# Stage seams of a hybrid decoder layer: order of the first tiles, who splits FFN2's first weights, and waits by chunk in the last down product

## What is computed

```
x = x + 0.5 * SwiGLU_1(rmsnorm(x))            # w_gate, w_up (1024 x 2816), w_down (2816 x 1024)
h = rmsnorm(x); p = h @ w_in                  # 72 column tiles of 128
A = sparse attention with an indexer's top-k; S = Mamba-2 SSD with gated RMSNorm
x = x + (sigmoid(ga) * (A @ w_attn_out) + sigmoid(gs) * (S @ w_ssd_out)) @ w_o
x = x + 0.5 * SwiGLU_2(rmsnorm(x))
```

## Time and profile before

| | |
|---|---|
| median of 3 runs | 3669.22 us (3666.39 to 3670.09) |
| the profiled execution | 3663.91 us |
| its span | 3661.7 us |
| PE busy | 3489.8 us, 95% |
| DVE busy | 2014.9 us, 55% |
| POOL busy | 1576.9 us, 43% |
| ACT busy | 764.0 us, 21% |
| mean granted clock of PE | 0.966 of 2.4 GHz |
| HBM | 74 GB/s over the span |

### The profile page before, as it was taken

How to read it: one execution, slowest core, us unless ns; L and a number is a source line. 1 busy time by engine, 2 the same in 40 slices (tenths; PEclk the granted TensorE clock), 3 DMA queues, 4 the chain that set the end, 5 groups by cost and what they waited for, 6 DMA issues and landing times.

```text
span 3661.7 us, 56375 instructions
## 1 busy us (share of the span) xinstructions
PE 3489.8 (95%) x22350; PEld 3271.4 (89%) x22350; DVE 2014.9 (55%) x2954; ACT 764.0 (21%) x1537; POOL 1576.9 (43%) x679
## 2 busy tenths in 40 slices
PE   7999999998999999999788889999999899999998
PEld 6999999988977999999667657779999899999998
DVE  5333333346666999987756636866273534334334
ACT  2000000012232111233665425651100200000000
POOL 3533433432322444444357417984443253353351
PEclk9999999999998999999799977999999999999999
DMA  2111111112211222232253326844151111111111
GB/s 85 56 46 34 53 50 34 52 40 76 56 29 58 92 91 91 79 98 92 67 53 105 106 67 176 233 119 150 49 172 50 29 58 40 40 57 40 40 57 52
DMA packets 399841, 272.29 MB, mean 74 GB/s; under 512 B 61843, under 2 KB 375523, under 8 KB 399721
## 3 DMA queue, kind: packets, MB, share of 16 engines
q1 hardware_dynamic: 379896, 225.75, 22.9%
q10 hardware_dynamic: 19824, 44.95, 3.3%
HBM read 211.05 MB, written 59.81 MB: 74 GB/s over the span
## 4 chain that ended last, share of the span: by engine, by line
PE 76%; DVE 15%; issue 3%; POOL 2%; ACT 1%; DMA 1%; another core or an unknown queue 0%; ACTq 0%; SPq 0%; DVEq 0%; POOLq 0%
PE setA L353 8%; PE setA L354 8%; PE setA L355 8%; PE setB L353 8%; PE setB L354 8%; PE setB L355 8%; DVE sc L1095 5%; DVE top L1093 5%; PE bankC L353 2%; PE bankC L355 2%; PE bankC L354 2%; PE bankD L355 2%; PE bankD L353 2%; PE bankD L354 2%; PE bankD L2054 1%
## 5 line engine op out<-in xcount | busy, mean ns | idle before, releaser
L345 POOL TENSOR_TENSOR whi<-wraw,ones 128x1024 fp32r<-128x1024 f32 x192 | 479.0, 2495 | 1669.6 <-PE setA L355 1095.3
L353 PE MATMUL setA<-hhi,whi 128*128 128x352 f32 (+1 forms) x2304 | 755.7, 328 | 40.0 <-POOL wlo L348 12.5
L353 PE MATMUL setB<-hhi,whi 128*128 128x352 f32 (+1 forms) x2304 | 750.0, 326 | 13.6 <-POOL wlo L348 13.6
L354 PE MATMUL setA<-hlo,whi 128*128 128x352 f32 (+1 forms) x2304 | 748.3, 325 | 0.0
L355 PE MATMUL setA<-hhi,wlo 128*128 128x352 f32 (+1 forms) x2304 | 747.1, 324 | 0.0
L354 PE MATMUL setB<-hlo,whi 128*128 128x352 f32 (+1 forms) x2304 | 745.3, 324 | 0.0
L355 PE MATMUL setB<-hhi,wlo 128*128 128x352 f32 (+1 forms) x2304 | 744.2, 323 | 0.0
L348 POOL TENSOR_TENSOR wlo<-wraw,whi 128x1024 fp32r<-128x1024 f32 x192 | 481.7, 2509 | 15.0
L353 PEld LDWEIGHTS setA<-hhi,whi 128*128 128x128 f32 x2304 | 438.6, 190 | 48.8 <-issue 30.6
L353 PEld LDWEIGHTS setB<-hhi,whi 128*128 128x128 f32 x2304 | 436.1, 189 | 18.2 <-POOL wlo L348 14.7
L354 PEld LDWEIGHTS setA<-hlo,whi 128*128 128x128 f32 x2304 | 438.5, 190 | 2.0
(11 more groups left out here) (413 smaller groups left out, 5503.8 us busy)
## 6 DMA issues: line engine op xcount, KB each, us to landing
wraw<-in_w_in SPq DMA_DIRECT2D x64, 512.0 KB, 3.7
wraw<-in_w_ffn_gate SPq DMA_DIRECT2D x44, 512.0 KB, 3.8
wraw<-in_w_ffn_up SPq DMA_DIRECT2D x44, 512.0 KB, 3.8
wraw<-in_w_ffn_down SPq DMA_DIRECT2D x44, 512.0 KB, 3.5
abc<-acsD SPq DMA_DIRECT2D x8, 2048.0 KB, 9.7
xcD<-cv ACTq DMA_DIRECT2D x24, 520.0 KB, 2.7
xc<-xcD SPq DMA_DIRECT2D x8, 1536.0 KB, 14.4
zD<-spill ACTq DMA_DIRECT2D x16, 524.0 KB, 2.7
```

The lines of the kernel that those rows point to most:

```text
L345: pool.tensor_tensor(dst_cols(slot, hi), dst_cols(slot), ones[:, :].unsqueeze(1).to_broadcast([P, KD, P]), ALU.mult).then_inc(w_hi, 1)
L353: pe.matmul(out, w1, r1, start=start, stop=False)
L354: pe.matmul(out, w1, r2, start=False, stop=False)
```

## The change

Four edits:

1. `gemm_pair` takes an order and the tile after which `between` is called. `after=0` in FFN1, FFN2 and w_in puts the sum of squares of chunk 2 between A0 and B0 instead of after B0.
2. In `pe_tail`, the first two tiles of both halves of w_ssd_out (s = 1, 2) run one after the other (A0 A1 A2 B0 B1 B2) by `gemm_tile`; those of w_o (s = 3) in the order A0 B0 A1 A2 B1 B2 (`FIRST_AHEAD`).
3. FFN2's first two weight tiles are split by ACT (`high_tile`, the rounded part) and DVE (`low_tile`, the rest) instead of POOL. ACT's two stand before and after the rounding of chunk 0, DVE's before and after its `hlo`. POOL waits until both are split and goes on with the third.
4. `pe_down_last` waits for the hidden tile chunk by chunk instead of for all of it.

```diff
--- before.py
+++ after.py
@@ -348,6 +348,18 @@
             pool.tensor_tensor(lo[:, slot, :], wraw[:, slot, :], hi[:, slot, :].bitcast(F32),
                                ALU.subtract).then_inc(w_split, 1)
 
+        def high_tile(act, n, half, slot, used):
+
+            act.wait_ge(raw_loaded[slot], half * 16 + 16)
+            act.wait_ge(*used)
+            act.activation(whi[:, slot, :], wraw[:, slot, :], ACT.Identity).then_inc(w_hi, 1)
+
+        def low_tile(v, n, slot):
+
+            v.wait_ge(w_hi, n + 1)
+            v.tensor_tensor(wlo[:, slot, :], wraw[:, slot, :], whi[:, slot, :].bitcast(F32),
+                            ALU.subtract).then_inc(w_split, 1)
+
         def products(pe, out, w1, w2, r1, r2, start, stop):
 
             pe.matmul(out, w1, r1, start=start, stop=False)
@@ -371,22 +383,24 @@
                     between(c)
 
 
-        def gemm_pair(pe, n, q, ready, between=None):
-
-            pe.wait_ge(w_split, n + 1)
-            for c, (o, w) in enumerate(CH):
-                if ready is not None:
+        ROUND = ((0, 0), (1, 0), (0, 1), (1, 1), (0, 2), (1, 2))
+        FIRST_AHEAD = ((0, 0), (1, 0), (0, 1), (0, 2), (1, 1), (1, 2))
+
+        def gemm_pair(pe, n, q, ready, between=None, order=ROUND, after=1):
+
+            for j, c in order:
+                o, w = CH[c]
+                if c == 0:
+                    pe.wait_ge(w_split, n + 1 + j)
+                if ready is not None and (j == 0 or order is not ROUND):
                     pe.wait_ge(ready[0], ready[1] + c + 1)
-                for j in range(2):
-                    if j and c == 0:
-                        pe.wait_ge(w_split, n + 2)
-                    if q:
-                        pe.wait_ge(gemm_evac[j], 3 * (q - 1) + c + 1)
-                    for k in range(KD):
-                        mm = products(pe, SETS[j][:, c, 0:w], whi[:, j, bass.ts(k, P)], wlo[:, j, bass.ts(k, P)],
-                                      hhi[:, k, o:o + w], hlo[:, k, o:o + w], k == 0, k == KD - 1)
-                    mm.then_inc(gemm_done[j], 1)
-                if between is not None:
+                if q:
+                    pe.wait_ge(gemm_evac[j], 3 * (q - 1) + c + 1)
+                for k in range(KD):
+                    mm = products(pe, SETS[j][:, c, 0:w], whi[:, j, bass.ts(k, P)], wlo[:, j, bass.ts(k, P)],
+                                  hhi[:, k, o:o + w], hlo[:, k, o:o + w], k == 0, k == KD - 1)
+                mm.then_inc(gemm_done[j], 1)
+                if between is not None and j == after:
                     between(c)
 
 
@@ -485,7 +499,11 @@
             act_square(act, r, 0)
             act_square(act, r, 1)
             act_root(act, r, 0)
+            if r == 2:
+                high_tile(act, TILE_FFN2, raw_count(TILE_FFN2), 0, (gemm_done[0], 3 * ORD_FFN2))
             act_round(act, r, 0)
+            if r == 2:
+                high_tile(act, TILE_FFN2 + 1, raw_count(TILE_FFN2 + 1), 1, (gemm_done[1], 3 * ORD_FFN2))
             act_square(act, r, 2)
             act_root(act, r, 1)
             act_round(act, r, 1)
@@ -565,7 +583,9 @@
 
         def pool_ffn(pool, f):
             n0, q0 = (TILE_FFN1, ORD_FFN1) if f == 0 else (TILE_FFN2, ORD_FFN2)
-            for j in range(4):
+            if f == 1:
+                pool.wait_ge(w_split, n0 + 2)
+            for j in range(0 if f == 0 else 2, 4):
                 q = q0 + j // 2
                 split_tile(pool, n0 + j, raw_count(n0 + j), j % 2, (gemm_done[j % 2], 3 * q) if q else None)
             if f == 1:
@@ -601,8 +621,8 @@
         def pe_down_last(pe, f, n, last_ready):
 
             pe.wait_ge(w_split, n + 2)
-            pe.wait_ge(hid_ready, last_ready)
             for c, (o, w) in enumerate(CH):
+                pe.wait_ge(hid_ready, last_ready - 2 + c)
                 for m in range(KD):
                     u = KD * c + m
                     if u >= 2:
@@ -618,7 +638,7 @@
 
         def pe_ffn(pe, f):
             n0, q0, r = (TILE_FFN1, ORD_FFN1, 0) if f == 0 else (TILE_FFN2, ORD_FFN2, 2)
-            gemm_pair(pe, n0, q0, (h_ready, 3 * r), (lambda c: pe_sumsq(pe, r, 2) if c == 0 else None))
+            gemm_pair(pe, n0, q0, (h_ready, 3 * r), (lambda c: pe_sumsq(pe, r, 2) if c == 0 else None), after=0)
             for j in range(2, 4):
                 gemm_tile(pe, n0 + j, q0 + j // 2, j % 2)
             with pe.Fori(0, NI - 1) as i:
@@ -842,7 +862,7 @@
                     split_tile(pool, i * 2 + (n0 + j), i + raw_count(n0 + 0) , j, (gemm_done[j], i * 3 + 3 * q0))
 
         def pe_in(pe):
-            gemm_pair(pe, TILE_IN, ORD_IN, (h_ready, 3), (lambda c: pe_sumsq(pe, 1, 2) if c == 0 else None))
+            gemm_pair(pe, TILE_IN, ORD_IN, (h_ready, 3), (lambda c: pe_sumsq(pe, 1, 2) if c == 0 else None), after=0)
             def tokens(first, last):
 
                 for t in range(first, last):
@@ -2368,7 +2388,11 @@
                 gemm_tile(pe, TILE_AO + m, ORD_AO + m // 2, m % 2)
             for s in (1, 2, 3):
                 n, q = (TILE_AO + 8 * s, PART_ORD[s])
-                gemm_pair(pe, n, q, (part_ready, 3 * s))
+                if s < 3:
+                    gemm_tile(pe, n, q, 0, ready=(part_ready, 3 * s))
+                    gemm_tile(pe, n + 1, q, 1)
+                else:
+                    gemm_pair(pe, n, q, (part_ready, 3 * s), order=FIRST_AHEAD)
                 with pe.Fori(0, 3 if s < 3 else 2) as i:
                     for j in range(2):
                         gemm_tile(pe, i * 2 + (n + 2 + j), i + (q + 1), j)
@@ -2495,7 +2519,9 @@
                         dve_scale(v, 2, 0, k)
                 for m in range(KD - 2, KD):
                     residual(m, c)
+            low_tile(v, TILE_FFN2, 0)
             dve_low(v, 2, 0)
+            low_tile(v, TILE_FFN2 + 1, 1)
             dve_norm(v, 2, ch, 1)
             dve_ffn(v, 1, ch)
             y_copy(v, 0)
```

## The result

Run beside the kernel before (median 3667.8 us, 3657.26 to 3670.09), the changed kernel has a median of **3621.52 us** (3614.41 to 3622.78): ratio 0.9873, 95% interval 0.9859 to 0.9888, or 46.3 us less. The forecast was 3632.5, its range 3617 to 3645. The time is in the range, 11 us from the forecast and 1.5 us from the rival "POOL gets in at s=1" (3623). The profiled execution of after took 3622.78 us.

A forecast was written before the change was run, and what follows sets the result against it. PE holds 76% of the chain that ended last, so gains come from its stops and low clock. Terms 8.0 + 2.3 + 1.5 + 0 + 10.1 + 1.4 + 13.4 = 36.7 us give 3632.5 us on the median, range 3617 to 3645.

The forecast's parts named there:

- `after=0`: FFN1 and w_in: the earlier sum of squares removes the third chunk's `hlo` stop, 4.0 us each (2.3 to 4.1).
- POOL gets in at s=1: Rival, w_ssd_out's first half: POOL splits between DVE's scalings, gaining 9.7 us there; total gain 46.4 us, 3623 us; chance 38%.
- s=2: Second half of w_ssd_out: sequence removes the stop before the second tile and another before the third; gain 10.1 us.
- s=3: w_o: the first tile ends one chunk earlier, covering PE's 1.32 us wait for the next tile's split; gain 1.4 us.
- FFN2's last down product: Waiting by chunk there wins back 1.5 us of a 1.6 us wait for `hidlo`.
- FFN2's weights: FFN2: without POOL, DVE's scalings shorten and the first tile starts 7.0 us earlier; gain 13.4 us (11.8 to 13.4).
- casts come too late: Rival at FFN2: late subtraction or `hlo` leaves the first tile's start unchanged, gain 4.0 instead of 13.4; 3642 us; chance 9%.
- kept out: w_ssd_out's first half: DVE's scalings hold up POOL's split, so the 5.8 us saved are waited one tile later; gain 0.
- Last down product of FFN1: Waiting by chunk starts PE earlier, then it stops about 4 us for bank C's copy; gain 2.3 us (1.6 to 3.0).
- the phase rule: w_ssd_out's first half: POOL's arrival time within a 0.50 us DVE operation decides whether it gets in; winning chance 45%.
- POOL is next when the operation ends: Skill's port rule at w_ssd_out's first half: waiting POOL follows the running DVE operation, gaining 9.7 us; the prediction did not adopt it.
- The low bound: FFN1's last down product: gain only 1.6 us if PE restarts at the low clock for 2.7 us.

The follow-up runs named there:

- e_sum: The kernel before with `after=0` alone, the sum of squares between the first two tiles of FFN1, w_in and FFN2: 3656.28 us, ratio 0.9959.
- a_lock: The changed kernel plus four GpSimd operations on an unused scratch tile where POOL split FFN2's weights before: 3631.81 us, ratio 0.9898.
- e_seq: The kernel before with only the first two tiles of both halves of w_ssd_out in sequence: 3652.73 us, ratio 0.9943.
- a_hid: The changed kernel with POOL's split of w_in's second tile held back until FFN1's `hidlo` is complete: 3619.58 us, ratio 0.9857.
- b_again: The kernel before, unchanged, profiled once more: 3671.87 us, ratio 1.0003.
- e_split: The kernel before with only FFN2's first two weight tiles split by ACT and DVE: 3663.93 us, ratio 0.9974.
- e_down: The kernel before with only the last down product waiting chunk by chunk: 3667.5 us, ratio 0.9992.
- a_pair: The changed kernel with the pairs in round order restored at both halves of w_ssd_out: 3643.86 us, ratio 0.9926.
- b_break6: The kernel before with one DVE self-wait in each stream of 24 scalings, after the 12th (first half) and 6th (second half): 3672.8 us, one run.
- b_break12: The kernel before with one DVE self-wait in each stream of 24 scalings, after the 15th (first half) and 12th (second half): 3671.15 us, one run.
- a_load: The changed kernel with two next weight tiles of w_ssd_out's first half loaded ahead of the half's large input `sraw`: 3611.77 us, ratio 0.9841.

## Why the prediction was right, and where it was not

**Terms that held.** `after=0` was put at 4.0 + 4.0; it gave 3.8 and 3.4, and e_sum shows both alone. s=2: 10.1 forecast, 10.2 measured. s=3: 1.4 and 1.4. FFN2's last down product: 1.5 and 1.5.

**FFN2's weights.** Forecast 13.4 (11.8 to 13.4), measured 12.1 on the means (7.2 to A, 4.9 behind it), 13.5 in the pair. ACT, DVE and PE in after, answering to the earlier trace rows:

```profile
2832.40 1.04 ACT L355 ACTIVATE whi<-wraw 128x1024 fp32r<-128x1024 f32 x1
...
2827.02 4.06 DVE L527 SCALAR_TENSOR_TENSOR hf<-X,g,rs 128x352 f32<-128x352 f32 x8
...
2832.03 1.22 DVE L360 TENSOR_TENSOR wlo<-wraw,whi 128x1024 fp32r<-128x1024 f32 x1
2833.16 3.15 DVE L537 TENSOR_TENSOR hlo<-hf,hhi 128x1408 fp32r<-128x1408 f32 x2
...
2836.42 0.40 PE L365 MATMUL setA<-hhi,whi 128*128 128x352 f32 x1
...
2865.54 0.43 PE L365 MATMUL setA<-hhi,whi 128*128 128x352 f32 x1 [1.31 <-POOL wlo L348]
```

The scalings are back at 4.06 us, the two estimates for the added work (1.05 and 1.2 us) came out at 1.04 and 1.22, and PE starts A without a stop. The 1.31 us that it waits for POOL's split at the third tile stand in before too (1.29 us) and take nothing off. The working started from the profile of before, in which A to third took 35.4 us, and against that profile it is right (13.4 and 13.5); the four unchanged profiles have 34.0 us on the mean (33.0 to 35.4), and that is the difference between 13.4 and 12.1. The rival "casts come too late" needed the first subtraction to be late; it is not. a_lock is the counter-test: the same order of ACT and DVE, with POOL back beside them, loses 6.4 of the 7.2 us.

**s=1: the failed step.** I took "kept out", gain 0, because POOL's arrival within the 0.50 us of one DVE operation seemed to decide. It gained 8.0 (8.4 on the means). It looks like no matter of chance: POOL got in at s=1 in all four profiles that have the sequence and the old place of the load (e_seq, after, a_hid, a_lock), and was kept out in all six with pairs and an unbroken stream (before, b_again, e_split, e_down, e_sum, a_pair). The timeline of DVE, the chain's DMA row and the timeline of PE in after answer to the earlier trace rows:

```profile
2559.38 20.31 DVE L2429 SCALAR_TENSOR_TENSOR sraw<-sraw,gssd,rs 128x352 f32<-128x352 f32 x24 [14.65 <-DMA sraw<-sD]
...
2545.17 15.80 DMA wraw<-in_w_ssd_out
...
2566.36 0.66 PE L365 MATMUL setA<-hhi,whi 128*128 128x352 f32 x1 [6.04 <-POOL wlo L348]
```

POOL came at 2561.12, 1.75 us behind the start of the stream, and took 2.52 us. What separates that from the 7.01 us of before is not the phase. This table takes the profiles of all the kernels, and in them every first operation of POOL after a standstill that met a running stream of DVE's scalings (all are `whi`, but for one of a_lock's scratch operations):

```
DVE operations since DVE's   met at phase                             DVE operations
last wait, at arrival        (us in the op)  times    POOL took, us    that passed it
2 to 6                       0.02 to 0.48       28    1.91 to 2.85    0 (once 1)
8 (b_break6)                 0.11, 0.33          2    4.68, 7.34      4, 10 (all left)
11 to 21                     0.02 to 0.49       20    4.14 to 9.03    3 to 13 (all left)
```

Both groups cover the whole period of an operation, so the phase rule falls. Nor does the number of operations that are still to come decide: with ten left, POOL got in in b_break12 and was passed by all ten in b_again, e_sum and a_pair. The count of operations since DVE last waited sorts all 50 cases. The two break kernels test it: they leave the place in the stream and the data alone and move only the wait. The limit lies between 6 and 8 operations, or, as the two go together, between 2.9 and 3.6 us. Two of the prediction's own rows fit: POOL at 2852.06 was at the second operation of its stream, POOL at 2568.30 at the 15th. I read these two as a matter of 0.3 us in phase where the position differed by 13 operations.

The same step cited the Trainium skill ("SBUF — State Buffer", "SBUF: two separate sides"), by which whoever starts first holds the port pair for its whole instruction. Within an operation the traces agree: POOL's `whi` took 2.82 us when it came 0.02 us into one (a_pair, at 2498.70) and 2.42 us when it came 0.41 us into one (e_down, at 2508.78), the rest of the 0.50 us being the difference. That POOL is next when the operation ends holds for 28 of the 50, and not for the 22 with a long run of DVE operations behind them. By which mechanism a stretch of such operations shuts POOL out, no run shows: that stays open.

Why 8.0 and not 9.7: A' was to start at 2568.2, with POOL arriving at 2563.0. The load took 15.80 us instead of 14.24, and that is 1.6 of the 1.7. (It took 15.7 to 15.9 us in all the other profiles with the old place of the load; the 14.24 of before was the exception.) Behind the stop of 6.04 us PE restarts at the lower clock, as it did in before behind 5.89 us, so that this costs nothing against before: third to fourth tile 13.9 us, and 13.7 there. Windows (us, busy us and instructions of PE, PEld, DVE, ACT, POOL, then PEclk, DMA share, GB/s):

```profile
2566.36:2571.00 4.64, 4.63 (x16) 4.64 (x17) 4.64 (x3) 0.00 (x0) 4.56 (x2) 0.50 0.38 113
2571.00:2575.00 4.00, 4.00 (x25) 4.00 (x24) 4.00 (x8) 0.47 (x1) 0.44 (x1) 0.94 0.45 131
```

At 0.16 us a matmul 4.64 us hold 29; 16 ran: 2.1 us, above the 1.1 to 1.6 that I took from the earlier trace rows. a_load removes stop and restart together: 6.2 us here (29.23 to 23.03) and 2.4 behind the third tile.

**Last down product of FFN1: the term that was mis-sized.** Forecast 2.3 (1.6 to 3.0), measured 0.2. The stop moved as told. Timelines of DVE and PE in after and a window, answering to the earlier trace rows:

```profile
781.96 2.15 DVE L677 CAST hidhi<-hidf 128x344 fp32r<-128x344 f32 x1
784.14 2.56 DVE L679 TENSOR_TENSOR hidlo<-hidf,hidhi 128x344 fp32r<-128x344 f32 x1
786.63 0.51 DVE L707 SCALAR_TENSOR_TENSOR X<-bankC,X 128x352 f32<-128x352 f32 x1
...
787.19 0.66 PE L365 MATMUL bankC<-hidhi,whid 128*128 128x352 f32 x1 [3.90 <-DVE X L707]
...
787.19:792.60 5.41, 5.41 (x18) 5.41 (x19) 1.43 (x3) 0.00 (x0) 0.00 (x0) 0.50 0.37 97
```

PE's stop went from 5.42 to 3.90 us, for bank C's copy behind `hidlo`: 1.5 us won. But the lower clock now lasts 5.4 us (18 matmuls where 34 fit, 2.6 us lost) where it was 3.4 us (12 where 21 fit, 1.4 lost): 1.2 us lost. The low bound was built on 2.7 us of low clock. That the lower clock follows from the new place of the stop is not shown, for both lengths come behind both stops. A window of a_pair, whose program is that of after up to here, behind the same stop of 3.90 us, and one of b_again, behind the same 5.42 us as in before:

```profile
786.14:789.40 3.26, 3.25 (x11) 3.26 (x12) 0.91 (x2) 0.00 (x0) 0.00 (x0) 0.50 0.61 161
```

```profile
789.87:795.20 5.33, 5.33 (x18) 5.33 (x19) 1.05 (x2) 0.00 (x0) 0.00 (x0) 0.50 0.37 98
```

From the end of the last hidden tile to w_in A the unchanged kernels took 43.8 to 43.9 us, whichever length they had; with the chunked wait it was 43.6 to 43.8 in after, e_down, a_load and a_lock, and 41.3 in a_pair, 2.5 us less than unchanged, near the 2.3 forecast. So 0.2 is the outcome of four profiles in five, and what decides between the two is open. a_hid shows the repair, in DVE's timeline, POOL's and a window:

```profile
781.08 0.34 DVE L677 CAST hidhi<-hidf 128x344 fp32r<-128x344 f32 x1
781.45 0.52 DVE L679 TENSOR_TENSOR hidlo<-hidf,hidhi 128x344 fp32r<-128x344 f32 x1
...
782.05 2.38 POOL L345 TENSOR_TENSOR whi<-wraw,ones 128x1024 fp32r<-128x1024 f32 x1 [5.88 <-DVE hidlo L679]
...
783.00:787.00 4.00, 4.00 (x27) 4.00 (x26) 1.96 (x4) 0.00 (x0) 3.83 (x2) 1.00 0.00 0
```

The whole stop was POOL's split of w_in's tile taking turns with DVE's cast and subtraction: 2.15 and 2.56 us with it, 0.34 and 0.52 without. With POOL starting 0.97 us behind the cast, where it was 0.44 us ahead of it, neither stop nor low clock is left.

**Ahead of w_o: a term that I did not have.** 4.8 us on the means. Timelines of POOL, DVE and PE, in b_again and in after:

```profile
2756.38 2.34 POOL L345 TENSOR_TENSOR whi<-wraw,ones 128x1024 fp32r<-128x1024 f32 x1 [6.53 <-PE setB L355]
...
2756.45 2.64 DVE L2475 TENSOR_TENSOR mixed<-mixed,acc 128x352 f32<-128x352 f32 x1
2759.02 5.25 DVE L2413 TENSOR_TENSOR hlo<-mixed,hhi 128x2816 fp32r<-128x2816 f32 x1
...
2764.37 0.63 PE L353 MATMUL setA<-hhi,whi 128*128 128x352 f32 x1 [8.14 <-issue]
```

```profile
2730.03 3.77 POOL L345 TENSOR_TENSOR whi<-wraw,ones 128x1024 fp32r<-128x1024 f32 x1 [6.54 <-PE setB L367]
...
2728.47 3.09 DVE L2437 TENSOR_TENSOR hlo<-mixed,hhi 128x2816 fp32r<-128x2816 f32 x1 [0.65 <-ACT hhi L2419]
...
2731.66 0.40 PE L365 MATMUL setA<-hhi,whi 128*128 128x352 f32 x1 [1.78 <-issue]
```

Where POOL starts first, DVE's `hlo` takes 5.08 to 5.25 us and PE stands 5.6 or 8.1 to 8.3 us; where DVE is first, `hlo` takes 3.09 and POOL pays, which no one waits for. With the sequence upstream DVE is first by 1.55 us in all six profiles that have it (70.9 us each). With the pairs POOL starts level with it or 0.1 to 2.8 us ahead: 72.5, 74.8 or 77.4 us (77.5 in b_break6). The longer `hlo` is only 2.0 to 2.2 us of this (nothing in before); the rest is that DVE comes to it later, by 1.6 us in before, 4.3 in b_again and 4.5 in b_break6, reckoned from s=2's third tile. In b_again the DVE operation ahead of it met the same split of POOL and took 2.64 us instead of 0.53. The prediction had only the profile of before, in which DVE and POOL start within 0.01 us of each other and DVE has the better of it. It was the cheapest of the unchanged ones. a_pair, which has all the other edits, stands at 74.8: it is the sequence that does it.

**The sum.** Forecast 36.7. To it come s=1 with 8.4 less 0.3, w_o's seam with 4.8, the end with 1.2 (where no edit stands) and s=2 with 0.1; off it go 2.1 at FFN1's last down product, 1.3 at FFN2 and 0.8 at `after=0`: 46.7, as measured on the means. The rival's 46.4 is near the truth by one right term (s=1) and by misses that cancel: the seam of w_o, not forecast, against the terms that were sized too high. The range held, since it was drawn out to that rival; the forecast's own range, 3628 to 3639, was missed. How close the total came to the rival's 3623 is luck: the seam of w_o and the end gave 6.0 us that no term had. (The lower ends of the terms add up to 31.0 us, not 30.9.) The rival's chance of 38% was too low, and it rested on the phase.

## What to carry to other kernels

Where GpSimd and VectorE work on SBUF at once, look at who starts first and how long VectorE has run without a wait, not only at who is busy. (The runs show the second for one kind of operation alone, scalings with two inputs in SBUF.) Move the GpSimd work off a seam (a_hid: 1.4 us later, 6.1 us gained), or break VectorE's run with a wait just ahead of the arrival. Where a small load stands behind a large one in an issuing queue and gates the next tile, issue it first: here one changed digit was worth 8.6 us in the stages and 9.7 between the medians.

## What I had not expected of the hardware

- A waiting GpSimd operation is passed by all that is left of a run of VectorE operations once eight or more of these have gone since VectorE's last wait (22 of 22; 4.1 to 9.0 us), and gets in when it comes by the sixth (28 of 28, 1.9 to 2.9 us). One self-wait turned 7 us into 2.6.
- Behind one and the same stop of PE the lower clock lasts two different times: behind 5.42 us it was 3.4 us in before and over 5.3 in b_again, behind 3.90 us with 12 matmuls ahead of it 5.4 us in after and 3.3 in a_pair. A sum that takes one row for the restart can be 2.5 us off.
- The weight tile issued right behind the 4192 KB of a half's input was 14.2 to 15.9 us on its way. The page's part 6 gives the 16 weight loads of this stage (KB, median us from issue to landing):

```profile
wraw<-in_w_ssd_out SPq DMA_DIRECT2D x16, 512.0 KB, 3.7
```
